# Feed-forward of a hybrid decoder: down products of two units in one PSUM sum, in two blocks per even unit

## The chip, the cores and the metric

The kernel runs on one core of a Trainium2 chip. Its time is device time in microseconds from the first to the last instruction, and what lies around it, of one execution. TensorE multiplies into PSUM (eight banks of 512 fp32 columns), VectorE, ScalarE and GpSimd do the element-wise work, and SyncE issues the DMAs. Each engine runs its own instructions in the order in which they are written and waits on semaphores.

## The reference, cut to what matters

The model layer is a token-mixing sub-layer and then the feed-forward (SwiGLU) that the change touches. T is 2056 tokens (2048 of the prompt, 8 samples), D is 1024, and the hidden width is 2816, 22 tiles of 128.

```python
h = _rmsnorm(x, g_pre_ffn) * (1.0 + sc_f) + sh_f
gate, up = jnp.split(jnp.einsum('btd,df->btf', h, w_ffn_in), 2, axis=-1)
f = jnp.einsum('btf,fd->btd', jax.nn.silu(gate) * up, w_ffn_out)
x = x + gt_f * _rmsnorm(f, g_post_ffn)
```

## The kernel before

The feed-forward is the last stage, `ffn`. Tokens stand in three groups of two halves (344, 342 and 342 tokens a half), and a group takes 22 **units**, one per tile of the hidden width, so units 0 to 65 in all; units 0 to 21 are group 0, 22 to 43 group 1, 44 to 65 group 2. The gate and up projections of a unit for both halves are made by a scheme of seven products instead of eight: `product` (L2094) does product j = 0 to 6 of a unit into the banks a, d, b, c, a, b, c, with 12 matmuls each, four chunks of the contraction times three terms of a high and a low part (`c_hi`, `c_lo` of the weights, `T_hi`, `T_lo` of the tokens).

What has to be ready for a product:

- VectorE makes four weight sums per unit, `s_add`: s3, s1, s2, s4 (L2269, L2272, L2276, L2280). ScalarE rounds each of the seven weight blocks to `c_hi` (`high_w`, L2137), GpSimd subtracts to get `c_lo` (`low_w`, L2034). Six buffers of each run ahead of TensorE.
- VectorE combines the products: `comb` (L2311) c11, u2, t, c22, u4, c21, c12. Product 5 writes bank b, so it waits for c11 of its own unit; product 6 waits for u2; product 4 waits for ScalarE's copy of product 0 (`first_product`); products 0 to 3 wait for t, u4, c21 and c12 of the unit ahead.
- ScalarE applies silu, VectorE multiplies (`gated`, L2317), ScalarE rounds to `f_hi` (`high_f`), VectorE makes `f_lo` (`low_f`, L2322). n is the half.
- The down weights of the unit are split the same way: `o_hi` on ScalarE (`high_o`, L2144), `o_lo` on GpSimd (`low_o`, L2039). Raw down weights have one buffer, loaded by SyncE when the `o_lo` ahead is done.

The down projection: unit d has 16 **tiles** y (eight rows of output tiles m, two halves n), each three matmuls into one of four banks Y (`tile`, L2112), which VectorE adds to `y` in SBUF (`collect`, L2339; a copy, L2337, for the first unit of a group). The tiles of unit d run in unit d+1, between the products (3, 3, 4, 3, 3 behind products 2 to 6). `spots` and `order`, built at the start of `ffn`, set this for all engines.

At a **turn** to the next group the new tokens h are loaded into the two buffers `E` and turned into seven `T` blocks in the last unit of the old group (t = 21, units 21 and 43) and the first of the new. In unit t = 1 of the new group there are no down tiles; instead the old group's `y` is squared into `E` (`squares`), summed by a tree on VectorE (`tree`), summed over partitions on TensorE (the two "sum" tiles), rooted on ScalarE (`root`), inverted, and scaled with `gate_f` (`scale`, L2394, eight instructions per half); then x is added (`output`, L2405) and SyncE stores the result. In t = 2 the tiles of two units run (6 behind most products). The same epilogue ends the kernel.

## Time and profile before

| | us |
|---|---|
| median of three runs | 2902.39 (2901.87 to 2910.81) |
| the profiled execution, its time | 2899.09 |
| its span, first to last instruction | 2897.0 |
| TensorE busy | 2566.6 (89%) |
| VectorE busy | 2109.5 (73%) |
| ScalarE busy | 1268.0 (44%) |
| GpSimd busy | 1270.5 (44%) |
| mean granted clock of TensorE | 0.953 of full speed |

The feed-forward starts its products at 1357 and ends its last tile at 2864, about half of the span. The busy time of TensorE counts a matmul until its modelled end, so two that overlap count once. An instruction's duration on VectorE, ScalarE and GpSimd includes the time in which it has been started and cannot yet proceed; the start of the next one lies up to 0.1 us ahead of its end.

### The profile page before, as it was taken

The numbers are of one execution on the slowest core, as the hardware profiler recorded it, in microseconds if no ns is written. First come the engines' busy times: TensorE is split into PE (matmuls) and PEld (weight loads), VectorE is DVE, ScalarE is ACT, GpSimd is POOL, SyncE is SP. The second block draws the span as 40 slices with busy tenths as digits, with TensorE's granted clock in tenths as the row PEclk, the third lists the DMA queues.
The fourth block names the chain that finished last, engine by engine and source line by source line (L and its number), as shares of the span: only waits on it lengthen the run. The fifth ranks groups of instructions, "written<-read, shape, count | busy, mean of one in ns | idle before, by whom it ended". The sixth has DMA issues, their size and how long they took to land. (4 is left out here: it accounts for less than half of the span.)

```text
span 2897.0 us, 43092 instructions
## 1 busy us (share of the span) xinstructions
PE 2566.6 (89%) x15492; PEld 2390.0 (83%) x15492; DVE 2109.5 (73%) x3246; ACT 1268.0 (44%) x2180; POOL 1270.5 (44%) x741
## 2 busy tenths in 40 slices
PE   5999999759888859995899999869999985999995
PEld 2999999647777747774899999759999975999995
DVE  2597789556767736744778777977777797777777
ACT  3556545357777744453333333423333342333332
POOL 1565566222323211001656555635656563555551
PEclk8999999979999979997999999989999998999997
DMA  5355344253333237953232222223222223222122
GB/s 217 117 174 168 130 149 168 80 123 94 79 101 95 57 100 214 278 170 113 79 106 83 71 79 75 71 103 119 74 81 73 81 66 107 81 66 88 67 74 85
DMA packets 199101, 315.40 MB, mean 109 GB/s; under 512 B 18210, under 2 KB 156194, under 8 KB 189938
## 3 DMA queue, kind: packets, MB, share of 16 engines
q1 hardware_dynamic: 174578, 295.80, 32.1%
q10 hardware_dynamic: 24320, 16.87, 2.2%
q8 instruction: 130, 2.13, 0.3%
q14 instruction: 73, 0.60, 0.1%
HBM read 266.29 MB, written 46.37 MB: 108 GB/s over the span
## 5 line engine op out<-in xcount | busy, mean ns | idle before, releaser
L2339 DVE TENSOR_TENSOR p_y<-p_y 128x342 f32<-128x342 f32 (+1 forms) x1008 | 462.6, 506 | 86.9 <-PE p_y L2112 86.9
L2034 POOL TENSOR_TENSOR p_c_lo<-ffn_wraw,p_c_hi 128x512 fp32r<-128x512 f32 x198 | 282.3, 1433 | 467.5 <-ACT p_c_hi L2137 467.5
L2034 POOL TENSOR_TENSOR p_c_lo<-p_graw,p_c_hi 128x512 fp32r<-128x512 f32 x198 | 275.1, 1396 | 324.4 <-ACT p_c_hi L2137 324.3
L2112 PE MATMUL p_y<-p_f_hi,p_o_hi 128*128 128x342 f32 (+1 forms) x1056 | 342.1, 324 | 72.1 <-DVE p_y L2337 48.3
L328 POOL TENSOR_TENSOR p_w_lo<-p_wraw,p_w_hi 128x1024 fp32r<-128x1024 f32 x100 | 294.9, 2958 | 212.2 <-ACT p_w_hi L389 211.9
L2112 PE MATMUL p_y<-p_f_hi,p_o_lo 128*128 128x342 f32 (+1 forms) x1056 | 340.5, 322 | 0.0
L2112 PE MATMUL p_y<-p_f_lo,p_o_hi 128*128 128x342 f32 (+1 forms) x1056 | 339.7, 322 | 0.0
L349 PE MATMUL p_proj<-p_h_hi,p_w_hi 128*128 128x412 f32 (+1 forms) x800 | 285.4, 357 | 15.3 <-POOL p_w_lo L328 15.2
L349 PE MATMUL p_proj<-p_h_lo,p_w_hi 128*128 128x412 f32 (+1 forms) x800 | 280.2, 350 | 0.0
L349 PE MATMUL p_proj<-p_h_hi,p_w_lo 128*128 128x412 f32 (+1 forms) x800 | 280.0, 350 | 0.0
L2112 PEld LDWEIGHTS p_y<-p_f_hi,p_o_hi 128*128 128x128 f32 x1056 | 201.3, 191 | 77.9 <-DVE p_y L2337 50.3
L2137 ACT ACTIVATE p_c_hi<-p_graw 128x512 fp32r<-128x512 f32 x198 | 120.2, 622 | 275.3 <-DVE p_graw L2276 197.7
L2137 ACT ACTIVATE p_c_hi<-ffn_wraw 128x512 fp32r<-128x512 f32 x198 | 120.2, 622 | 267.4 <-DVE ffn_wraw L2276 200.8
L2155 ACT ACTIVATE p_cg<-p_cg 128x342 f32<-128x342 f32 (+1 forms) x132 | 64.9, 491 | 322.8 <-DVE p_cg L2311 322.8
L2112 PEld LDWEIGHTS p_y<-p_f_lo,p_o_hi 128*128 128x128 f32 x1056 | 201.2, 191 | 0.0
L2112 PEld LDWEIGHTS p_y<-p_f_hi,p_o_lo 128*128 128x128 f32 x1056 | 201.2, 191 | 0.0
L2094 PE MATMUL p_a<-p_T_hi,p_c_hi 128*128 128x342 f32 (+1 forms) x528 | 171.5, 325 | 22.3 <-DVE p_T_lo L2364 16.4
L2322 DVE TENSOR_TENSOR p_f_lo<-p_cg,p_f_hi 128x342 fp32r<-128x342 f32 (+1 forms) x132 | 146.8, 1112 | 59.5 <-ACT p_f_hi L2162 59.5
L2039 POOL TENSOR_TENSOR p_o_lo<-ffn_wraw,p_o_hi 128x1024 fp32r<-128x1024 f32 x66 | 178.2, 2701 | 12.6 <-ACT p_o_hi L2144 12.6
L2094 PE MATMUL p_c<-p_T_hi,p_c_hi 128*128 128x342 f32 (+1 forms) x528 | 171.4, 325 | 9.1 <-POOL p_c_lo L2034 7.2
L2094 PE MATMUL p_b<-p_T_hi,p_c_hi 128*128 128x342 f32 (+1 forms) x528 | 170.2, 322 | 7.8 <-DVE p_cg L2311 6.1
L2094 PE MATMUL p_c<-p_T_lo,p_c_hi 128*128 128x342 f32 (+1 forms) x528 | 171.6, 325 | 0.0
(312 smaller groups left out, 7088.9 us busy)
## 6 DMA issues: line engine op xcount, KB each, us to landing
p_wraw<-w_in SPq DMA_DIRECT2D x100, 512.0 KB, 4.7
p_graw<-w_ffn SPq DMA_DIRECT2D x33, 1024.0 KB, 5.0
ffn_wraw<-w_ffn SPq DMA_DIRECT2D x65, 512.0 KB, 3.5
...
```

The source lines that it names most:

```text
L328: pool.tensor_tensor(w_lo[s][:], wraw[:, s, :], w_hi[s][:].bitcast(F32), ALU.subtract).then_inc(lo_done, 1)
L349: mm = pe.matmul(proj[n % 2][:, 0:W], a[n % RW][:, ks], b[g % 2][:, k, 0:W], start=i == 0, stop=i == 3 * KT - 1)
L2034: pool.tensor_tensor(c_lo[r][:], source(p), c_hi[r][:].bitcast(F32), ALU.subtract).then_inc(S["lo"], 1)
L2039: pool.tensor_tensor(o_lo[u % 2][:], oraw, o_hi[u % 2][:].bitcast(F32), ALU.subtract).then_inc(S["olo"], 1)
L2094: mm = pe.matmul(out[:, 0:W], a[r][:, k, :], b[j][:, k, 0:W], start=i == 0, stop=i == 11)
L2112: mm = pe.matmul(Y[q % YB][:, 0:W], a[s][:, m, :], b[s][:, n, 0:W], start=i == 0, stop=i == 2)
L2137: act.activation(c_hi[p % NR][:], source(p), ACT.Copy).then_inc(S["hi"], 1)
L2155: act.activation(cg[n][:, 0:W], cg[n][:, 0:W], ACT.Silu).then_inc(S["silu"], 1)
L2322: dve.tensor_tensor(f_lo[u % 2][:, n, 0:W], cg[n][:, 0:W], f_hi[u % 2][:, n, 0:W].bitcast(F32), ALU.subtract).then_inc(S["f"], 1)
L2339: dve.tensor_tensor(to, to, part, ALU.add).then_inc(S["yadd"], 1)
```

## The change

The down tiles of two units are one sum in PSUM: a tile of the pair u-2, u-1 is six matmuls in one bank, three per unit, and VectorE adds it to `y` once. All 16 tiles of a pair run in the even unit u, eight (half 0) behind product 5 and eight (half 1) behind product 6; an odd unit has none. The 16 tiles of the last pair run behind the last product. The high part of the down weights of an even unit is made at the start of the next unit, since its buffer is read until the end of the block; that of an odd unit is made ahead of `high_f`. At the turn, the two sums over partitions move behind products 3 and 6 of t = 1; the factor `gate_f` is taken to ScalarE (`gate`, eight instructions per half); `scale` is two VectorE instructions per half and `output` two; the first root moves behind the c_hi 2 of the next unit, the second root, inverse, scale and output go to t = 2; the two stores of y are issued in t = 1 and t = 2, one each.

```diff
     def pieces(u):
-        return [0, 2, 6, 6, 6, 6, 6] if len(downs(u)) == 2 else [0, 0, 3, 3, 4, 3, 3]
+        if u % 2 or not u:
+            return [0] * NPR
+        return [0, 0, 0, 0, 0, 8, 8]
...
+        pair = [("y", u - 2, n, m) for n in range(2) for m in range(KT)]
+        counts = pieces(u) if u < NU4 else [2 * KT]
+        for j, c in enumerate(counts):
+            spots[u, j] = list(range(len(order), len(order) + c))
+            order += pair[sum(counts[:j]):sum(counts[:j]) + c]
+            if u % FT == 1 and u > FT and j in (3, 6):
                 spots[u, j].append(len(order))
-                order.append(x)
...
+                order.append(("sum", group(u) - 1, (3, 6).index(j)))
...
                 if t == 0 and G:
                     for n in range(2):
                         load_x(G - 1, n)
-                    for n in range(2):
-                        store_y(G - 1, n)
+                if t in (1, 2) and G:
+                    store_y(G - 1, t - 1)
...
+                if u % 2:
+                    low_o(u - 1)
                 low_w(NPR * u + 5)
...
                 low_w(NPR * (u + 1) + 4)
-                low_o(u)
+                if u % 2:
+                    low_o(u)
...
-                    W, s = HW[group(d)], d % 2
-                    wait_f(pe, d, "lo", n)
-                    pe.wait_ge(S["olo"], d + 1)
-                    for i, (a, b) in enumerate(((o_hi, f_hi), (o_hi, f_lo), (o_lo, f_hi))):
-                        mm = pe.matmul(Y[q % YB][:, 0:W], a[s][:, m, :], b[s][:, n, 0:W], start=i == 0, stop=i == 2)
+                    W = HW[group(d)]
+                    for s in range(2):
+                        wait_f(pe, d + s, "lo", n)
+                        pe.wait_ge(S["olo"], d + s + 1)
+                        for i, (a, b) in enumerate(((o_hi, f_hi), (o_hi, f_lo), (o_lo, f_hi))):
+                            mm = pe.matmul(Y[q % YB][:, 0:W], a[s][:, m, :], b[s][:, n, 0:W], start=s == 0 and i == 0,
+                                           stop=s == 1 and i == 2)
...
+            def gate(G, n):
+                WP = HW[G] - (NS if G == NGR - 1 and n == 1 else 0)
+                act.wait_ge(S["sq"], 2 * G + n + 1)
+                for k in range(KT):
+                    ins = act.activation(y[:, k, n, 0:WP], y[:, k, n, 0:WP], ACT.Copy, scale=mods["gate_f"][:, k, 0:1])
+                ins.then_inc(S["gate"], 1)
...
-                high_o(u)
...
-                for k in range(KT):
-                    ins = dve.scalar_tensor_tensor(out=y[:, k, n, 0:WP], in0=y[:, k, n, 0:WP],
-                                                   scalar=mods["gate_f"][:, k, 0:1], in1=rstd[n][:, 0:WP],
-                                                   op0=ALU.mult, op1=ALU.mult)
...
+                dve.wait_ge(S["gate"], 2 * G + n + 1)
+                for k in (0, 4):
+                    dve.tensor_tensor(y[:, k:k + 4, n, 0:W], y[:, k:k + 4, n, 0:W],
+                                      rstd[n][:, 0:W].unsqueeze(1).broadcast_to((P, 4, W)), ALU.mult).then_inc(S["ep"], 1)
```

The line numbers of the changed kernel are a little higher: L2285 to L2296 are the weight sums (before L2269 to L2280), L2327 the combinations, L2333 the gate product, L2338 f_lo, L2353 the copies of y. On GpSimd the order of the instructions is the same in both kernels; what moves is what they wait for.

VectorE in a steady unit of group 0, from the gate product of half 0 (behind c21) on. Before:

```order
L2317 TENSOR_TENSOR p_cg<-p_cg,p_tt 128x344
L2339 TENSOR_TENSOR p_y<-p_y 128x344 x3
L2322 TENSOR_TENSOR p_f_lo<-p_cg,p_f_hi 128x344
L2311 TENSOR_TENSOR p_cg<-p_pu,p_c 128x344
L2339 TENSOR_TENSOR p_y<-p_y 128x344 x3
L2317 TENSOR_TENSOR p_cg<-p_cg,p_up 128x344
L2322 TENSOR_TENSOR p_f_lo<-p_cg,p_f_hi 128x344
L2280 TENSOR_TENSOR p_graw<-p_graw 128x512
L2269 TENSOR_TENSOR p_s<-ffn_wraw 128x512
L2339 TENSOR_TENSOR p_y<-p_y 128x344 x3
L2272 TENSOR_TENSOR ffn_wraw<-ffn_wraw 128x512
```

After, the same place in unit 2, whose tiles are the group's first and so copies:

```order
L2333 TENSOR_TENSOR p_cg<-p_cg,p_tt 128x344
L2353 COPY p_y<-p_y 128x344 x8
L2338 TENSOR_TENSOR p_f_lo<-p_cg,p_f_hi 128x344
L2327 TENSOR_TENSOR p_cg<-p_pu,p_c 128x344
L2353 COPY p_y<-p_y 128x344 x8
L2333 TENSOR_TENSOR p_cg<-p_cg,p_up 128x344
L2338 TENSOR_TENSOR p_f_lo<-p_cg,p_f_hi 128x344
L2296 TENSOR_TENSOR p_graw<-p_graw 128x512
L2285 TENSOR_TENSOR p_s<-ffn_wraw 128x512
L2288 TENSOR_TENSOR ffn_wraw<-ffn_wraw 128x512
L2327 TENSOR_TENSOR p_cg<-p_pu,p_b 128x344
```

The y instructions stand in two runs of eight behind the gate product and behind c12, and none are left between s3 and s1 or between the combinations.

ScalarE in a steady pair, from silu of half 0 on. Before, one unit:

```order
L2155 ACTIVATE p_cg<-p_cg 128x344
L2137 ACTIVATE p_c_hi<-p_graw 128x512 x3
L2162 ACTIVATE p_f_hi<-p_cg 128x344
L2137 ACTIVATE p_c_hi<-p_s 128x512
L2144 ACTIVATE p_o_hi<-ffn_wraw 128x1024
L2155 ACTIVATE p_cg<-p_cg 128x344
L2137 ACTIVATE p_c_hi<-p_graw 128x512
L2150 ACTIVATE p_pu<-p_a 128x344
```

After, from silu of half 0 of an even unit (no `o_hi` in it) to the start of the next:

```order
L2156 ACTIVATE p_cg<-p_cg 128x344
L2138 ACTIVATE p_c_hi<-p_graw 128x512 x3
L2163 ACTIVATE p_f_hi<-p_cg 128x344
L2138 ACTIVATE p_c_hi<-p_s 128x512
L2156 ACTIVATE p_cg<-p_cg 128x344
L2145 ACTIVATE p_o_hi<-ffn_wraw 128x1024
L2138 ACTIVATE p_c_hi<-p_graw 128x512
L2151 ACTIVATE p_pu<-p_a 128x344
L2163 ACTIVATE p_f_hi<-p_cg 128x344
L2138 ACTIVATE p_c_hi<-p_graw 128x512
```

`o_hi` of the even unit now stands behind the silu of the next unit's start, ahead of the c_hi 5, `p_pu` (product 0) and `f_hi` of half 1.

VectorE at the first turn, unit 23 (t = 1). Before, from s1 on:

```order
L2272 TENSOR_TENSOR ffn_wraw<-ffn_wraw 128x512
L2381 RECIPROCAL p_rstd<-p_rstd 128x344
L2311 TENSOR_TENSOR p_cg<-p_pu,p_b 128x342
L2311 TENSOR_TENSOR p_pu<-p_pu,p_c 128x342
L2394 SCALAR_TENSOR_TENSOR p_y<-p_y,gate_f,p_rstd 128x344 x8
L2311 TENSOR_TENSOR p_tt<-p_pu,p_a 128x342
L2311 TENSOR_TENSOR p_up<-p_tt,p_d 128x342
L2311 TENSOR_TENSOR p_pu<-p_pu,p_d 128x342
```

After, from t on, so with what stood there before further down:

```order
L2327 TENSOR_TENSOR p_tt<-p_pu,p_a 128x342
L2327 TENSOR_TENSOR p_up<-p_tt,p_d 128x342
L2327 TENSOR_TENSOR p_pu<-p_pu,p_d 128x342
L2397 RECIPROCAL p_rstd<-p_rstd 128x344
L2292 TENSOR_TENSOR ffn_wraw<-ffn_wraw 128x512
L2327 TENSOR_TENSOR p_tt<-p_tt,p_b 128x342
L2333 TENSOR_TENSOR p_cg<-p_cg,p_tt 128x342
L2404 TENSOR_TENSOR p_y<-p_y,p_rstd 128x4x344 x2
L2338 TENSOR_TENSOR p_f_lo<-p_cg,p_f_hi 128x342
L2418 TENSOR_TENSOR p_E<-p_E,p_y 128x1376 x2
L2327 TENSOR_TENSOR p_cg<-p_pu,p_c 128x342
```

The inverse and the scaling of half 0 move from around c11 and u2 to behind u4 and the gate product; the scaling is two instructions, the output two.

## Rows read from the trace of the kernel before

**Rows 1.** Page, the span in 40 equal slices: TensorE's busy tenths.

```profile
PE   5999999759888859995899999869999985999995
```

**Rows 2.** Windows: length, busy us (instructions) per engine, clock, DMA share, GB/s.

```profile
1812.82:1869.58 56.76, 46.27 (x265) 45.16 (x265) 50.48 (x71) 23.54 (x34) 34.16 (x19) 0.91 0.16 56
1869.58:1948.44 78.86, 48.07 (x270) 45.01 (x269) 62.88 (x91) 25.24 (x36) 34.13 (x18) 0.85 0.34 116
2321.85:2378.28 56.43, 46.00 (x265) 44.87 (x265) 50.51 (x71) 23.56 (x34) 34.21 (x19) 0.91 0.16 57
2378.28:2461.66 83.38, 47.17 (x270) 44.13 (x269) 62.74 (x90) 25.08 (x36) 33.98 (x18) 0.84 0.39 109
2461.66:2482.35 20.69, 20.69 (x134) 20.69 (x133) 15.65 (x32) 6.25 (x12) 9.65 (x8) 1.00 0.18 63
2355.04:2378.28 23.24, 21.29 (x134) 20.75 (x133) 22.83 (x35) 10.77 (x17) 16.86 (x11) 1.00 0.21 70
```

**Rows 3.** Waits of TensorE, 1200 to 2897: us in total, times, longest.

```profile
PE p_y L2112 <- DVE p_y L2337: 48.3, 6, 13.5
```

**Rows 4.** Timeline of VectorE, first turn: start, us, what, [idle before <-releaser].

```profile
1834.85 2.88 DVE L2364 TENSOR_TENSOR p_T_lo<-p_E,p_T_hi 128x1368 fp32r<-128x1368 f32 x1 [2.19 <-ACT p_T_hi L2175]
...
1859.64 0.50 DVE L2311 TENSOR_TENSOR p_cg<-p_pu,p_b 128x342 f32<-128x342 f32 x1
...
1885.43 0.45 DVE L2311 TENSOR_TENSOR p_cg<-p_pu,p_b 128x342 f32<-128x342 f32 x1
...
1886.41 6.05 DVE L2394 SCALAR_TENSOR_TENSOR p_y<-p_y,gate_f,p_rstd 128x344 f32<-128x344 f32 x8
...
1922.89 0.69 DVE L2269 TENSOR_TENSOR p_s<-p_graw 128x512 f32<-128x512 f32 x1 [8.43 <-DMA p_graw<-w_ffn]
```

**Rows 5.** Timeline of SyncE's queue, first turn.

```profile
1900.98 13.24 SPq L2004 DMA_DIRECT2D yT<-p_E  x2
```

**Rows 6.** Timeline of VectorE, a steady unit of group 2.

```profile
2515.56 0.51 DVE L2311 TENSOR_TENSOR p_tt<-p_pu,p_a 128x342 f32<-128x342 f32 x1 [1.35 <-PE p_a L2094]
...
2517.01 1.76 DVE L2339 TENSOR_TENSOR p_y<-p_y 128x342 f32<-128x342 f32 x4
```

**Rows 7.** Timeline of ScalarE, the same stretch.

```profile
2505.21 0.46 ACT L2150 ACTIVATE p_pu<-p_a 128x342 f32<-128x342 f32 x1 [1.22 <-PE p_a L2094]
...
2520.49 0.49 ACT L2162 ACTIVATE p_f_hi<-p_cg 128x342 fp32r<-128x342 f32 x1 [0.39 <-DVE p_cg L2317]
...
2520.89 0.62 ACT L2137 ACTIVATE p_c_hi<-p_s 128x512 fp32r<-128x512 f32 x1
...
2521.41 1.04 ACT L2144 ACTIVATE p_o_hi<-ffn_wraw 128x1024 fp32r<-128x1024 f32 x1
```

**Rows 8.** Timeline of TensorE, first matmul of a steady unit.

```profile
2503.12 0.32 PE L2094 MATMUL p_a<-p_T_hi,p_c_hi 128*128 128x342 f32 x1
```

**Rows 9.** Timeline, VectorE and GpSimd (POOL) side by side in unit 1.

```profile
1398.53 2.67 POOL L2039 TENSOR_TENSOR p_o_lo<-ffn_wraw,p_o_hi 128x1024 fp32r<-128x1024 f32 x1
...
1399.64 1.94 DVE L2322 TENSOR_TENSOR p_f_lo<-p_cg,p_f_hi 128x344 fp32r<-128x344 f32 x1 [0.69 <-ACT p_f_hi L2162]
...
1401.17 1.56 POOL L2034 TENSOR_TENSOR p_c_lo<-p_graw,p_c_hi 128x512 fp32r<-128x512 f32 x1
...
1401.51 1.77 DVE L2280 TENSOR_TENSOR p_graw<-p_graw 128x512 f32<-128x512 f32 x1
...
1403.20 0.68 DVE L2269 TENSOR_TENSOR p_s<-ffn_wraw 128x512 f32<-128x512 f32 x1
```

**Rows 10.** Timeline of GpSimd (POOL), a steady unit of group 2.

```profile
2513.05 2.54 POOL L2034 TENSOR_TENSOR p_c_lo<-ffn_wraw,p_c_hi 128x512 fp32r<-128x512 f32 x2 [2.42 <-ACT p_c_hi L2137]
```

**Rows 11.** Timeline of TensorE, unit 23, product 5.

```profile
1886.02 0.40 PE L2094 MATMUL p_b<-p_T_hi,p_c_hi 128*128 128x342 f32 x1 [2.37 <-DVE p_cg L2311]
```

**Rows 12.** Timeline of VectorE at the end of the kernel.

```profile
2864.82 1.58 DVE L2370 TENSOR_TENSOR p_E<-p_E 128x1368 f32<-128x1368 f32 x1
...
2873.04 3.98 DVE L2394 SCALAR_TENSOR_TENSOR p_y<-p_y,gate_f,p_rstd 128x342 f32<-128x342 f32 x8
```

More of the change, by code:

```diff
@@ L1888, in ffn @@
         if x[0] == "y":
-            done[x[1]], done[x[1], x[2]] = q + 1, q + 1
+            for d in (x[1], x[1] + 1):
+                done[d], done[d, x[2]] = q + 1, q + 1
     with ExitStack() as ctx:
@@ L1925, in ffn @@
         E_LOADS = {("h", 0): 1, ("h", 1): 2, ("x", 0): 3, ("h", 2): 4, ("x", 1): 5, ("x", 2): 6}
-        S = {n: sem(n) for n in ("prod", "tile", "hi", "ohi", "p1", "silu", "fhi", "thi", "sq", "root", "s_add", "comb", "f",
+        S = {n: sem(n) for n in ("prod", "tile", "hi", "ohi", "p1", "silu", "fhi", "thi", "sq", "gate", "root", "s_add", "comb", "f",
                                  "yadd", "t_dve", "ep", "lo", "olo", "t_pool")}
@@ L2215, in _ @@
                     squares(G - 1, 1)
+                if G and t == 2:
+                    root(G - 1, 1)
                 first_product(u)
@@ L2229, in _ @@
                 if G and t == 1:
-                    root(G - 1, 0)
+                    gate(G - 1, 0)
                 silu(u, 0)
@@ L2239, in _ @@
                     high_t(turn, 3)
+                if G and t == 1:
+                    root(G - 1, 0)
                 high_w(NPR * (u + 1) + 3)
@@ L2242, in _ @@
                     high_t(turn, 4)
-                if G and t == 1:
-                    root(G - 1, 1)
+                if u % 2:
+                    high_o(u)
                 high_f(u, 0)
                 high_w(NPR * (u + 1) + 4)
-                high_o(u)
+                if G and t == 1:
+                    gate(G - 1, 1)
                 if turn:
@@ L2255, in _ @@
                 squares(NGR - 1, n)
+                gate(NGR - 1, n)
             for n in range(2):
@@ L2404, in output @@
                 dve.wait_ge(e_in[n], 16 * E_LOADS["x", G])
-                dve.tensor_tensor(E[n][:, :, 0:W], E[n][:, :, 0:W], y[:, :, n, 0:W], ALU.add).then_inc(S["ep"], 1)
+                if G == NGR - 1 and n == 1:
+                    ys = y[:, :, n, W - NS:W]
+                    dve.tensor_tensor(ys, ys, mods["gate_f"][:, :, 1:C9], ALU.mult).then_inc(S["ep"], 1)
+                    wait_ep(dve, G, f"part{n}")
+                    dve.tensor_tensor(E[n][:, :, 0:W], E[n][:, :, 0:W], y[:, :, n, 0:W], ALU.add).then_inc(S["ep"], 1)
+                else:
+                    for k in (0, 4):
+                        dve.tensor_tensor(E[n][:, k:k + 4, 0:W], E[n][:, k:k + 4, 0:W], y[:, k:k + 4, n, 0:W], ALU.add
+                                          ).then_inc(S["ep"], 1)
             low_t(0, 0)
@@ L2429, in _ @@
                     inverse(late, 1)
-                    scale(late, 1)
                 collect(u, 0)
@@ L2441, in _ @@
                 if late is not None:
-                    output(late, 1)
+                    scale(late, 1)
                 collect(u, 1)
@@ L2453, in _ @@
                 s_add(u + 1, "s1")
-                if ends is not None:
-                    inverse(ends, 0)
+                if late is not None:
+                    output(late, 1)
                 comb(u, "c11")
@@ L2462, in _ @@
                     low_t(0, 6)
-                if ends is not None:
-                    scale(ends, 0)
                 comb(u, "t")
@@ L2467, in _ @@
                 comb(u, "u4")
+                if ends is not None:
+                    inverse(ends, 0)
                 collect(u, 4)
@@ L2473, in _ @@
                 gated(u, 0)
+                if ends is not None:
+                    scale(ends, 0)
                 collect(u, 5)
```

34 lines of the change are left out of this document (7 added, 27 removed).

## The prediction

> **What bounds the kernel now.** I read the span in slices first: TensorE is busy in nine tenths or more of most of the second half, where the feed-forward runs, with two dents [rows 1]. The windows say how full: a steady unit of group 2 takes 20.69 us, TensorE and its weight load are both busy for all 20.69 us, at a granted clock of 1.00 [rows 2]. A unit has 84 matmuls for seven products and 48 for the down tiles, so one takes 20.69/132 = 0.157 us. Nothing that VectorE saves can shorten such a unit. What can be gained is in the two dents, the turns from one token group to the next. The four units of the first turn (21 to 24) take 56.76 + 78.86 = 135.6 us, those of the second 56.43 + 83.38 = 139.8 us [rows 2], against 4 x 20.75 = 83 us of TensorE work. The largest waits there are the 48.3 us for the copies of the new group's first tiles, which stand on VectorE behind the outputs of the old group [rows 3]. Between the copies VectorE waited 8.43 us for weights [rows 4], whose load SyncE could issue only after it had stood in two stores of y for 13.24 us [rows 5].
>
> **Work that stays and work that goes.** TensorE does the same matmuls: 528 tiles of six for 1056 of three. The 528 removed VectorE additions at 0.42 us from start to start (four from 2517.01, the last ending at 2518.77 with 0.08 us of overlap [rows 6]) are some 220 us of an engine that a steady unit does not wait for: worth nothing by themselves. In an even unit (from here w) all tiles stand behind products 5 and 6, so a unit is no longer an even 20.7 us: an odd unit v is 84 x 0.157 = 13.2 us, an even one 180 x 0.157 = 28.2 us. VectorE, ScalarE and GpSimd still have the same preparation per unit, and until now the tiles gave it time. So I follow the preparation through a pair, with 0 at the first matmul of v. A product starts every 1.88 us, and its result can be used 2.09 us after its first matmul (2503.12 to 2505.21 [rows 7, 8]).
>
> **The pair, step by step.** VectorE and GpSimd stand in each other's way: f_lo takes 1.94 us where o_lo runs on GpSimd, and ends 0.4 us after it. The weight sum that follows (L2280) takes 1.77 us beside a c_lo, against 0.68 us for its neighbour [rows 9]. In the Trainium skill, "SBUF — State Buffer", section "Who interferes with whom", such an instruction with two SBUF inputs waits for the whole GpSimd instruction, and one with a PSUM input does not. By that the removed additions (one PSUM input each) give GpSimd nothing; if they had shared its port, some 0.4 us a tile would have come back to it, which the sum here does not hold.
> ScalarE splits o of the last even unit at 0.2 to 1.2 (1.04 us [rows 7]), GpSimd makes its o_lo until 3.7 (2.67 us in a row that begins with some 0.3 us of waiting [rows 9]). f_lo ends at 4.1, s4 (behind a c_lo) at 5.8, s3 and s1 follow, and c11 of v is there at 7.6. TensorE wants it for product 5 at 5 x 1.88 = 9.4: cover of 1.8 us. The result of product 4 comes at 9.6; t, c22 and u4 follow, and s2 starts 1.45 us later, at 11.1 (2515.56 to 2517.01 [rows 6]). GpSimd is then inside a run of four c_lo, 1.25 us each (two in 2.54 [rows 10]), until 12.0, so s2 ends at 12.5. c21 and the gate product follow (13.6), on ScalarE c_hi 3, o_hi of v (1.04 us, now ahead of f_hi) and f_hi (14.6), then c_hi 4 (15.1); on VectorE f_lo (15.1) and c12 (15.6). silu ends at 16.1, the second gate product waits for c_lo 4 (16.8), and o_lo of v runs until 19.1. From the end of an o_lo to c11 the rows give 2.0 us (1401.20 to 1403.20 [rows 9]) and then s3, s1 and c11, 1.8 us: c11 of w is there at 22.9, and TensorE starts 0.14 us after it (1885.88 to 1886.02 [rows 4, 11]), at 23.0. It wants it at 12 x 1.88 = 22.6. So **0.4 us are lost in each pair**, and what hides the rest of the chain is used up. 28 of the 32 even units with tiles are outside the turns: 28 x 0.4 = +11 us. The bounds: 0 us where s2 slips in ahead of the c_lo (then c11 comes 1.1 us earlier), and 1.1 us a pair where one more c_lo (1.25 us) gets in ahead of s1: 0 to +31 us. Within w the tiles come every 0.94 us and VectorE needs 0.42 for one, so four banks are enough.
>
> **The turns.** First half, units 21 and 22. VectorE bounds them already, with the new group's T. In front of c11 of unit 22 (it ends at 1860.1, 47.3 us after the start of 21 [rows 2, 4]) 19 y adds go, 19 x 0.42 = 8.0 us. But part of them filled waits for ScalarE's T_hi (2.19 us before T_lo at 1834.85 [rows 4]), and f_lo and s4 at the start of 21 now meet o_lo (2.4 us more); following the chain as above, c11 comes at 45 us. Now, though, all 96 tile matmuls and products 5 and 6 stand behind it: 120 x 0.157 = 18.9 us, where 9.5 us stood (56.76 less 47.3). The clock adds to this: TensorE is busy for 46.27 us in the first half [rows 2], where 264 matmuls at 0.157 are 41.4, so 4.8 us go at half clock. I take 1.5 of them behind c11. This is 65.5 us for 56.6: +9 us in each turn.
> Second half, units 23 and 24. What goes: the load is no longer behind the second store, the copies stand behind products 5 and 6, and scaling changes from eight instructions of 6.05 us in all [rows 4] to two, for which the nearest row is an add of the same size, 1.58 us [rows 12], so 3.2 us and a c_lo of 1.25 on top. What comes: eight ScalarE instructions per half (8 x 0.40 = 3.2 us, from start to start as f_hi at 2520.49 and what follows it at 2520.89 [rows 7]), which put the first root from 16 to 19 us. The chain is then: c11 of 23 at 15.5; root at 19, reciprocal 2.3, s2, c21, gate product, scale 4.4, f_lo, output 4.3 with a c_lo: c12 at 32; second root at 35, reciprocal 2.3, f_lo, s4, scale 4.4, s3, s1, output 4.3: c11 of 24 at 49.3. With 18.9 us of TensorE work and 1.8 at half clock that is 70 us, for 78.86 and 83.38: -9 and -13 us. **Both turns together: 9 + 9 - 9 - 13 = -4 us.** The bounds: -25 us, where the 8 us of adds and the scales' 3 us come out in full in every half; +15 us, where each wait meets one more c_lo on its way.
>
> **Start and end.** Units 0 and 1 keep their order but for the tiles, which units 1 and 2 exchange: 0. At the end the root waits 3.2 us for the gate copies, of which the squares' sum hid half, and two scales save 2 x (3.98 - 3.16) [rows 12]: 0.
>
> **Sum.** 11 - 4 + 0 = +7 us on the profiled execution of 2899.09 us, which is 3.3 us below the median; on the median, 2902.4 + 7 = 2909 us. A measurement of this kernel can tell some 0.3% (8.7 us) from no change.
>
> **Rivals.**
> Forecast, about no change (2894 to 2911): the shortfall of 0.4 us a pair and turns that give a little. For it speaks that every piece has a row; against it that it is a difference of two long chains. Chance 0.40.
> Slower: one mechanism, the wait of product 5 in each even unit for c11, which stands on VectorE behind o_lo. If one c_lo more gets in, the loss is 1.1 to 1.6 us a pair: 28 x 1.4 = 39, less 4: 2937 us. It decides from (8.7 + 4)/28 = 0.45 us a pair on. For it speaks that two c_lo and an o_lo lie in the chain and each missed turn costs 1.25 us; against it that s1 is ready 0.15 us before the next c_lo. Chance 0.30.
> Faster: steady pairs lose nothing and the turns give 25 us, since VectorE, busy for 62.88 of 78.86 us there [rows 2], gets rid of its adds and long scales: 2878 us. For it speaks that half of the wait at the turns was for a load that comes earlier now; against it that tiles at the end of a unit no longer fill TensorE's waits. Chance 0.25.
> Slower still: the clock. From 2355.04 to 2378.28 TensorE was idle for 23.24 - 21.29 = 1.95 us in short pieces, at a clock of 1.00 [rows 2], so short waits did not cost it there. If a wait in each pair does bring it down, at half of the 4.8 us from above for each, it is 28 x 2.4 = 67 us: 2974 us. Chance 0.05. "TensorE: Matmul & The Clock Gate", section "A second HAM failure mode: psum-queue depth-cycling" of the Trainium skill, describes such a clock that swings with small idle times between groups; no row here shows it.
>
> **Chances.** Faster 0.25, same 0.40, slower 0.35. The range has to reach to both neighbours: 2878 to 2942 us.
>
> **What would show it.** Right: even units of about 28.6 us with TensorE's wait for p_cg (c11) of 0.4 us at product 5; odd units of 13.2 us without a wait; units 21 and 22 together 65 us, 23 and 24 together 70 us; VectorE's busy time down by some 250 us. Wrong: a wait of over 1 us a pair, or none; a wait in odd units (for c_lo 5 or s1); turns under 120 us; a clock under 1.00 in a steady stretch.

## The result: 0.3% slower, and where the time went

The changed kernel takes 2912.95 us (median, 2906.52 to 2917.46) against 2902.31 us (2896.56 to 2910.81) of the kernel before: the ratio is 1.0034, with a 95% interval of 1.0026 to 1.0042. The forecast was 2909 us, with 2878 to 2942 us as its range. The difference, 10.6 us, is a little more than the 8.7 us that the prediction called the smallest that a measurement of this kernel can tell from none, and the interval leaves no doubt of its sign. The median lies 2 us above the band that the prediction gave its likeliest case (2894 to 2911 us). One of the five executions of the kernel e4_unpaired below took 4333.8 us at a granted clock of 0.554; its ratio is that of the other four, whose median is 2935.58 us.

The page of the changed kernel begins as follows (span; busy us of each engine; TensorE's busy tenths in 40 slices, which answer to [rows 1]):

```profile
span 2912.4 us, 42580 instructions
...
PE 2581.5 (89%) x15492; PEld 2401.1 (82%) x15492; DVE 2018.1 (69%) x2686; ACT 1289.3 (44%) x2228; POOL 1297.5 (45%) x741
...
PE   5999999759888959995999999779999977999995
```

VectorE does 560 instructions less and TensorE is no better used. The windows below answer to [rows 2] (length, busy us of TensorE, its weight load, VectorE, ScalarE and GpSimd with instructions, granted clock, DMA share, GB/s): units 21 and 22, units 23 and 24, the same of the second turn, then an odd and an even steady unit.

```profile
1821.56:1884.91 63.35, 46.52 (x265) 45.47 (x265) 48.42 (x55) 25.29 (x34) 34.92 (x18) 0.87 0.15 50
1884.91:1955.48 70.57, 49.54 (x270) 48.39 (x269) 57.90 (x62) 30.20 (x49) 30.54 (x16) 0.83 0.32 105
2336.19:2399.58 63.39, 45.80 (x266) 44.79 (x265) 48.33 (x55) 25.27 (x34) 34.61 (x18) 0.89 0.16 51
2399.58:2470.39 70.81, 50.64 (x270) 49.49 (x269) 57.83 (x62) 30.16 (x49) 30.49 (x16) 0.81 0.33 104
2470.39:2483.66 13.27, 13.27 (x87) 13.27 (x85) 9.45 (x14) 5.63 (x10) 9.35 (x6) 1.00 0.67 155
2483.66:2512.59 28.93, 28.54 (x181) 28.28 (x181) 20.84 (x33) 8.57 (x17) 15.53 (x10) 1.00 0.26 88
```

A steady pair is 13.27 + 28.93 = 42.20 us, where two units took 41.49 us before (2482.35 to 2523.84, start to start). By stretches, from the start of unit 1 to the last instruction of each profiled execution, in us:

| stretch | before | after | difference | predicted |
|---|---|---|---|---|
| units 1 to 20 | 416.46 | 422.37 | +5.9 | |
| units 25 to 42 | 373.41 | 380.71 | +7.3 | |
| units 47 to 64 | 373.41 | 379.76 | +6.4 | |
| steady, together | | | +19.6 | +11 |
| units 21+22, 43+44 | 56.76, 56.43 | 63.35, 63.39 | +13.5 | +18 |
| units 23+24, 45+46 | 78.86, 83.38 | 70.57, 70.81 | -20.9 | -22 |
| unit 65 to the end | 61.93 | 62.25 | +0.3 | 0 |
| sum | 1500.64 | 1513.21 | +12.6 | +7 |

Ahead of unit 1 the code is unchanged but for the place of o_hi and o_lo of unit 0; in the profiled executions of all kernels of this study unit 1 begins between 1392.2 and 1401.9 us, so the 2.8 us by which it begins later here lie within that spread and are not counted to the change.

TensorE's waits in the feed-forward, which answer to [rows 3] (us in total, times, longest):

```profile
PE p_b L2093 <- DVE p_cg L2327: 63.5, 37, 10.4
PE p_c L2093 <- DVE p_cg L2327: 21.7, 4, 6.0
PE p_a L2093 <- DVE p_tt L2327: 3.3, 2, 1.8
```

The 48.3 us of waits for copies are gone entirely. In their place stand waits of product 5 (bank b) for c11, 37 of them: one in each of the 28 steady even units, eight at the turns and one in unit 0. At the turns there are also four of product 3 (bank c) for c12.

### The profile page after: what moved, and what is told of

It reads as the page before. It is cut to its first block and busy times, and to the rows that moved or that the text cites. A ratio compares the mean times of both kernels' runs of the same rounds, so it can differ in the third digit from the quotient of the medians.

```text
span 2912.4 us, 42580 instructions
## 1 busy us (share of the span) xinstructions
PE 2581.5 (89%) x15492; PEld 2401.1 (82%) x15492; DVE 2018.1 (69%) x2686; ACT 1289.3 (44%) x2228; POOL 1297.5 (45%) x741
## 5 line engine op out<-in xcount | busy, mean ns | idle before, releaser
L2030 POOL TENSOR_TENSOR p_c_lo<-ffn_wraw,p_c_hi 128x512 fp32r<-128x512 f32 x198 | 285.8, 1456 | 293.5 <-ACT p_c_hi L2138 293.5
L2355 DVE TENSOR_TENSOR p_y<-p_y 128x342 f32<-128x342 f32 (+1 forms) x480 | 237.2, 509 | 145.1 <-PE p_y L2112 143.2
L2030 POOL TENSOR_TENSOR p_c_lo<-p_graw,p_c_hi 128x512 fp32r<-128x512 f32 x198 | 302.6, 1548 | 62.2 <-ACT p_c_hi L2138 62.2
L2093 PE MATMUL p_b<-p_T_hi,p_c_hi 128*128 128x342 f32 (+1 forms) x528 | 176.7, 335 | 65.1 <-DVE p_cg L2327 63.5
L2338 DVE TENSOR_TENSOR p_f_lo<-p_cg,p_f_hi 128x342 fp32r<-128x342 f32 (+1 forms) x132 | 142.6, 1080 | 105.6 <-ACT p_f_hi L2163 103.3
L2093 PE MATMUL p_c<-p_T_hi,p_c_lo 128*128 128x342 f32 (+1 forms) x528 | 173.5, 329 | 0.0
```

Of the source, the lines that this page charges most:

```text
L2030: pool.tensor_tensor(c_lo[r][:], source(p), c_hi[r][:].bitcast(F32), ALU.subtract).then_inc(S["lo"], 1)
L2093: mm = pe.matmul(out[:, 0:W], a[r][:, k, :], b[j][:, k, 0:W], start=i == 0, stop=i == 11)
L2338: dve.tensor_tensor(f_lo[u % 2][:, n, 0:W], cg[n][:, 0:W], f_hi[u % 2][:, n, 0:W].bitcast(F32), ALU.subtract).then_inc(S["f"], 1)
L2355: dve.tensor_tensor(to, to, part, ALU.add).then_inc(S["yadd"], 1)
```

## Experiments

All medians are beside runs of the kernel before on the same chip. "Pair" is an odd and an even steady unit of the later groups (two units where the tiles are spread over both). Units are given for the first turn and the second.

| kernel | median, us | ratio, 95% interval | pair, us | 21+22, 43+44 | 23+24, 45+46 |
|---|---|---|---|---|---|
| changed | 2912.95 | 1.0034 (1.0026 to 1.0042) | 42.20 | 63.35, 63.39 | 70.57, 70.81 |
| e1_olo_late | 2918.24 | 1.0057 (1.0044 to 1.007) | 42.27 | 64.78, 64.83 | 70.28, 69.59 |
| e9_short_olo | 2892.69 | 0.9975 (0.9963 to 0.9986) | 41.57 | 62.48, 62.52 | 68.83, 68.56 |
| e4_unpaired | 2936.35 | 1.012 (1.0103 to 1.0136) | 43.11 | 63.50, 63.40 | 68.13, 68.02 |
| e2_tiles_early | 2883.68 | 0.9941 (0.9927 to 0.9956) | 41.50 | 61.33, 61.35 | 66.93, 66.84 |
| e8_no_gate | 2882.95 | 0.9944 (0.993 to 0.9958) | 41.50 | 61.31, 60.96 | 67.77, 67.50 |
| e6_old_tiles | 2886.35 | 0.9957 (0.9944 to 0.9971) | 41.49 | 56.81, 56.46 | 70.25, 71.69 |
| e5_before_stores | 2878.01 | 0.9921 (0.9908 to 0.9934) | 41.49 | 56.79, 56.37 | 69.75, 69.12 |
| e13_four_ahead | 2873.92 | 0.9894 (0.9878 to 0.9911) | 41.49 | 56.77, 56.38 | 68.05, 68.17 |
| e10_pairs_at_turn | 2862.26 | 0.9865 (0.9848 to 0.9882) | 41.49 | 56.77, 56.44 | 62.44, 62.27 |
| e11_late_epilogue | 2877.10 | 0.9917 (0.9903 to 0.9932) | 41.49 | 56.80, 56.38 | 69.90, 69.71 |
| e12_tiles_later | 2853.54 | 0.9844 (0.983 to 0.9858) | 41.49 | 56.75, 56.38 | 58.05, 59.47 |

### The steady pair: o_lo placed later

```diff
                 low_w(NPR * u + 6)
+                if u and u % 2 == 0:
+                    low_o(u - 1)
...
                 low_w(NPR * (u + 1) + 4)
-                if u % 2:
-                    low_o(u)
+            low_o(NU4 - 1)
```

> The changed kernel, with o_lo of the odd unit placed behind c_lo 6 of the even unit instead of behind c_lo 4 made for it, so that f_lo (half 1) and s4 no longer stand behind it on the way to c11. Theory (the steady loss is the wait of product 5 for c11, and o_lo is what makes c11 late): c11 of the even unit is there at about 21 to 22 us of a pair, wanted at 22.6; the wait of 0.39 us is gone, a pair takes 41.6 us instead of 42.2, and 28 pairs give 17 us: about 2896 us. Rival (the o_lo meets another instruction with two SBUF inputs on the same way, such as s3 or s1, and the wait stays): 2913 us within 4. If only the wait goes and the rest of the excess is in the blocks themselves: 28 x 0.4 = 11 us, 2902 us.

It got slower: 2918.24 us. The first half of the theory came true, the second not. VectorE, GpSimd and TensorE in the even unit that starts at 2534.16:

```profile
2541.25 0.50 DVE L2328 TENSOR_TENSOR p_cg<-p_pu,p_b 128x342 f32<-128x342 f32 x1
...
2546.21 1.69 DVE L2293 TENSOR_TENSOR p_graw<-p_graw 128x512 f32<-128x512 f32 x1 [0.95 <-POOL p_c_lo L2030]
...
2549.35 2.31 DVE L2356 TENSOR_TENSOR p_y<-p_y 128x342 f32<-128x342 f32 x5
```

```profile
2542.44 2.42 POOL L2035 TENSOR_TENSOR p_o_lo<-ffn_wraw,p_o_hi 128x1024 fp32r<-128x1024 f32 x1
2544.80 5.76 POOL L2030 TENSOR_TENSOR p_c_lo<-p_graw,p_c_hi 128x512 fp32r<-128x512 f32 x4
```

```profile
2549.90 0.42 PE L2113 MATMUL p_y<-p_f_hi,p_o_hi 128*128 128x342 f32 x1 [0.52 <-DVE p_y L2356]
```

c11 ends at 2541.75, 20.85 us into the pair (21 to 22 expected), and product 5 no longer waits. But s2 waits for GpSimd (0.95 us, for a c_lo) and starts 12.05 us into the unit, and the first addition of the block starts at 15.19. In the changed kernel these are 11.94 and 15.01 us, so VectorE's row hardly moved, while TensorE now begins the block 11.26 us into the unit instead of 11.89. The fifth tile wants a bank that the first addition has to free, and now waits 0.52 us. The wait moved from the front of the block into it.

### The steady pair: o_lo made short

```diff
-                pool.tensor_tensor(o_lo[u % 2][:], oraw, o_hi[u % 2][:].bitcast(F32), ALU.subtract
-                                   ).then_inc(S["olo"], 1)
+                part = slice(0, 1) if u % 2 and u > 1 else slice(0, KT)
+                pool.tensor_tensor(o_lo[u % 2][:, part, :], oraw[:, part, :], o_hi[u % 2][:, part, :].bitcast(F32),
+                                   ALU.subtract).then_inc(S["olo"], 1)
```

> The changed kernel in which o_lo of the odd units is made for one of its eight blocks only (about 0.35 us of GpSimd instead of 2.67 us; the other seven keep the values of unit 1, so that part of the output leaves out the low part of the down weights as it should be); nothing else is changed. Theory (the loss of 0.63 to 0.7 us in each steady pair is GpSimd's o_lo, which makes either c11 or, where it stands later, the first addition late): c11 of the even unit at about 20.7 us of a pair, no wait at product 5 and none in the block, 41.55 us a pair, about 18 us less than the changed kernel: 2895 us. Rival (VectorE's own row of instructions is too long between the start of the even unit and the first addition, whatever GpSimd does): a wait in the block of 0.4 us or more stays, 2908 us or more.

2892.69 us (2895 expected). A steady pair, columns as in the windows above:

```profile
2447.09:2488.66 41.57, 41.57 (x266) 41.57 (x265) 27.86 (x46) 14.19 (x26) 22.69 (x16) 1.00 0.41 110
```

TensorE is busy for the whole pair: no wait at product 5 and none in the block. With the run before this one it says that the wait of a steady pair is the odd unit's o_lo, 2.67 us of GpSimd in front of f_lo and s4 or in front of s2. In neither of the two places tried for it are both c11 and the first addition on time, with all tiles behind product 5; other places were not tried.

### The order without the sum

```diff
-        return [0, 0, 0, 0, 0, 8, 8]
+        return [0, 0, 0, 0, 0, 16, 16]
...
-        pair = [("y", u - 2, n, m) for n in range(2) for m in range(KT)]
+        pair = [("y", d, n, m) for n in range(2) for d in (u - 2, u - 1) for m in range(KT)]
```

(and `tile` makes three matmuls of one unit again.)

> The changed kernel with tiles of three matmuls again, 16 behind product 5 and 16 behind product 6 of the even unit, each added by VectorE: the order of the change without the sum of two units. Theory A (the additions that the pairing saves are hidden in a steady pair, as the 0.157 us for each of 132 matmuls said, and cost only at the turns): about 2913 + 2 x 7 = 2927 us. Theory B (with tiles of 0.47 us the four banks are full 1.9 us after the block begins, while VectorE comes to the first addition only at 28.3 us of the pair, 3.1 us after the block's start; so TensorE waits about 1.8 us in each pair): 2913 + 28 x 2 + 14 = about 2983 us. So the two-unit sum and the blocks would be worth something only together.

2936.35 us: between the two theories. A pair takes 43.11 us, 0.9 us more than with the sum; the wait is in the block, as Theory B had it, and of about the size that it named, 1.45 us for 1.8. That theory forgot that the wait at product 5 (0.39 us in the profile) goes when the block is longer: the steady units have none here, and c11 is there 22.1 us into the pair, not 23.0.

```profile
2509.01 0.43 PE L2111 MATMUL p_y<-p_f_hi,p_o_hi 128*128 128x342 f32 x1 [1.45 <-DVE p_y L2353]
```

So in blocks at the end of a unit the sum is worth some 23 us. That is a balance: the steady stretches are 27.7 us longer without it, but units 23+24 and 45+46 are 2.4 and 2.8 us shorter (68.13 and 68.02 for 70.57 and 70.81), where both theories took the missing sum to cost time; why was not followed. In the steady pairs the sum repairs a loss that the blocks make; against tiles spread over the unit it gains nothing there (41.49 us without blocks and without sums).

### The same tiles, four of them ahead of product 5

```diff
-        return [0, 0, 0, 0, 0, 8, 8]
+        return [0, 0, 0, 2, 2, 6, 6]
```

> The changed kernel with the tiles of the even unit as 2, 2, 6 and 6 behind products 3, 4, 5 and 6, instead of 8 and 8 behind 5 and 6: TensorE has 24 matmuls (3.8 us) more to do before product 5 wants c11. Theory: the steady wait goes (28 x 0.6 = 17 us), and at the turns four tiles fill 3.8 us of the waits of 1.1 and 10.4 us for c11 (1 + 4 us in each turn, 10 us in both): about 2886 us. Rival (what counts is VectorE's chain at the turns, which gets four additions more ahead of t and s2): the steady gain alone, about 2896 us. Rival (the steady excess isn't the wait): above 2903 us.

2883.68 us (2886 expected), 0.6% faster than the kernel before. Units 21+22, units 23+24, and a steady pair:

```profile
1814.10:1875.43 61.33, 46.31 (x266) 45.54 (x265) 47.24 (x55) 25.40 (x34) 34.34 (x18) 0.86 0.16 52
1875.43:1942.36 66.93, 49.90 (x270) 48.74 (x269) 56.66 (x62) 30.19 (x49) 30.29 (x16) 0.85 0.34 111
2457.21:2498.71 41.50, 41.50 (x267) 41.50 (x266) 30.20 (x46) 14.18 (x27) 24.25 (x16) 1.00 0.32 103
```

The 24 matmuls ahead of product 5 cover c11, the pair has no wait, and the turns are 2.0 us (21+22) and 3.6 us (23+24) shorter, since TensorE has tiles while it waits. VectorE's instructions are the same in number: only places changed.

### The stores alone

```diff
                 if t == 0 and G:
                     for n in range(2):
                         load_x(G - 1, n)
-                    for n in range(2):
-                        store_y(G - 1, n)
+                if t in (1, 2) and G:
+                    store_y(G - 1, t - 1)
```

> The kernel before, with the two stores of y issued in t = 1 and t = 2, behind the loads of the weights, as in the changed kernel; nothing else is changed. Theory (at the turn the copies wait for s3, and s3 for a load that SyncE issues behind the second store): VectorE's waits of 8.4 and 14.1 us for the load go, and the two units t = 1 and 2 take 71 and 70 us for 78.9 and 83.4: about 2902 - 20 = 2882 us. So the turns' gain of the change (8.3 and 12.6 us in those units) would come from the stores alone. Rival (behind the load another wait is late, c_hi and c_lo of the next unit): a gain of under 10 us, 2893 us or more.

2878.01 us: 22.8 us less than before, by two DMA instructions put elsewhere. Units 23+24 and 45+46, and the place on VectorE at which it waited 8.43 us for the load [rows 4]:

```profile
1869.75:1939.50 69.75, 46.87 (x270) 44.22 (x269) 63.04 (x91) 25.03 (x36) 34.50 (x18) 0.90 0.35 110
2369.31:2438.43 69.12, 49.21 (x270) 46.73 (x269) 62.93 (x91) 24.99 (x36) 34.47 (x18) 0.88 0.36 109
```

```profile
1914.14 0.50 DVE L2337 COPY p_y<-p_y 128x342 f32<-128x342 f32 x1
1914.56 0.92 DVE L2269 TENSOR_TENSOR p_s<-p_graw 128x512 f32<-128x512 f32 x1
```

s3 follows the copy with no wait. The two stretches are 9.1 and 14.3 us shorter than before, and 0.8 and 1.7 us shorter than in the changed kernel. So this line alone is enough for all that the change gained at the turns (20.9 us; the line gives 23.4). The changed kernel with the stores in their old place was not run.

### The change's epilogue with the tiles of before

Changed kernel; `pieces`, `order`, `tile`, `high_o` and `low_o` as before:

```diff
-        return [0, 0, 0, 0, 0, 8, 8]
+        return [0, 2, 6, 6, 6, 6, 6] if len(downs(u)) == 2 else [0, 0, 3, 3, 4, 3, 3]
...
-                if u % 2:
-                    low_o(u)
+                low_o(u)
```

> The changed kernel with the tiles of the kernel before: tiles of three matmuls of one unit, 3, 3, 4, 3, 3 behind products 2 to 6 of the next unit, both o_hi and o_lo in their old places; the epilogue (sums, gate on ScalarE, roots, scale, output, stores) stays as changed. Theory (the change's epilogue is good for the turns and its tiles are bad for them and for the steady pairs): pairs of 41.5 us, units 21+22 56.8 us as before, units 23+24 about 66 us: 41.49 x 28 and turns of 123 us, 6 us less than with the stores alone: about 2872 us. Rival (the epilogue gives nothing beyond the stores, since VectorE adds 32 tiles again in t = 2): 2878 to 2882 us. Rival (the tiles of two units cost the turns, not the place of the tiles): units 23+24 at 70 us as in the changed kernel, 2880 us.

2886.35 us: the first rival, and a little worse than it (2878 to 2882). Units 21+22 take 56.81 us, so the 6.6 and 7.0 us that the change loses there come from its tiles and the places of o_hi and o_lo that go with them. Units 23+24 take 70.25 us, no less than with the stores alone, and the stretch from unit 65 to the end is 3.4 us longer than there, which was not followed. The second root now stands in t = 2 and holds a bank of the tiles:

```profile
1905.52 0.66 PE L2113 MATMUL p_y<-p_f_hi,p_o_hi 128*128 128x342 f32 x1 [8.20 <-ACT p_rstd L2202]
```

### The factor gate_f back on VectorE

Kernel with 2, 2, 6, 6, without `gate`:

```diff
-                for k in (0, 4):
-                    dve.tensor_tensor(y[:, k:k + 4, n, 0:W], y[:, k:k + 4, n, 0:W],
-                                      rstd[n][:, 0:W].unsqueeze(1).broadcast_to((P, 4, W)), ALU.mult).then_inc(S["ep"], 1)
...
+                for k in range(KT):
+                    ins = dve.scalar_tensor_tensor(out=y[:, k, n, 0:WP], in0=y[:, k, n, 0:WP],
+                                                   scalar=mods["gate_f"][:, k, 0:1], in1=rstd[n][:, 0:WP],
+                                                   op0=ALU.mult, op1=ALU.mult)
...
```

> The kernel with tiles 2, 2, 6, 6 behind products 3 to 6, with the scaling by gate_f back on VectorE (eight instructions per half, none on ScalarE). Theory (the gate copies on ScalarE hide nothing that VectorE would have had to do later: two scales save 0.9 us each in clean time, and the first root comes up to 1.2 us later for them): the same as the kernel with the gate copies, 2884 us within 3. Rival (ScalarE's factor is what shortens the second half of the turn): 2 turns x 4 us, 2892 us.

2882.95 us, the same as 2883.68 within the intervals. Units 23+24 take 67.77 us for 66.93, and the stretch from unit 65 to the end 61.56 us for 61.95: a small gain at each turn that the end gives back in part.

### The sum only where VectorE is the bound

Two kernels, both from the one with the stores moved. The first:

```diff
-        return [0, 2, 6, 6, 6, 6, 6] if len(downs(u)) == 2 else [0, 0, 3, 3, 4, 3, 3]
+        return [0, 1, 3, 3, 3, 3, 3] if len(downs(u)) == 2 else [0, 0, 3, 3, 4, 3, 3]
...
-        todo = [("y", d, n, m) for d in downs(u) for n in range(2) for m in range(KT)]
+        todo = [("y", d, n, m) for d in downs(u)[:1] for n in range(2) for m in range(KT)]
```

(and a tile of unit 22 or 44 is six matmuls, three of it and three of the unit behind it.)

> The kernel before with the stores moved, and the sum of two units only in the two units t = 2 of the turns (units 24 and 46), where the tiles of t = 0 and t = 1 run together: 1, 3, 3, 3, 3, 3 tiles of six matmuls behind products 1 to 6 instead of 2, 6, 6, 6, 6, 6 of three. Everywhere else a tile is one unit. Theory (the sum is worth something only where VectorE, not TensorE, sets the end): in a turn 16 additions of 0.43 us go (some of them hidden behind TensorE), and the four banks hold 3.8 us of TensorE work instead of 1.9 us when it comes to wait for the first copy: units t = 1 and 2 take 66 us instead of 69.6, 6 to 7 us in all: about 2872 us. Rival (behind the first copy TensorE's own work sets the end, and the additions are hidden here too): 1.9 us a turn or less, 2874 to 2878 us.

2862.26 us, ratio 0.9865: more than expected, 15.7 us less than with the stores alone. Unit 24 there, then here:

```profile
1893.20:1939.50 46.30, 31.67 (x180) 30.50 (x181) 40.24 (x63) 13.61 (x22) 22.04 (x12) 0.85 0.23 70
```

```profile
1894.38:1933.36 38.98, 31.07 (x180) 30.26 (x181) 32.73 (x48) 11.65 (x19) 19.28 (x10) 0.91 0.24 77
```

VectorE is busy for 7.5 us less (15 instructions), and the unit is 7.3 us shorter. The second kernel keeps the places and leaves the sum out:

```diff
-        return [0, 2, 6, 6, 6, 6, 6] if len(downs(u)) == 2 else [0, 0, 3, 3, 4, 3, 3]
+        return [0, 1, 3, 7, 7, 7, 7] if len(downs(u)) == 2 else [0, 0, 3, 3, 4, 3, 3]
```

> The kernel before with the stores moved, and the 32 tiles of t = 2, still of three matmuls each, as 1, 3, 7, 7, 7, 7 behind products 1 to 6 instead of 2, 6, 6, 6, 6, 6: the same four tiles stand ahead of product 3 as in the run with pairs at the turn, and only the sum of two units is missing. That run gained 15.7 us on the moved stores, against 6 to 7 expected. Theory A (the removed additions did it: behind the first copy VectorE has 32 of 0.43 us and some 9 us of other work, 23 us, against 17 us of TensorE work; so VectorE sets the end here and 16 additions are 7 us a turn): this run gains 0 to 2 us a turn, 2874 to 2878 us. Theory B (the places did it: TensorE makes product 3 while it waits, and starts less cold): 2862 to 2866 us.

```profile
1895.45:1940.03 44.58, 32.11 (x181) 29.89 (x182) 39.76 (x63) 13.61 (x22) 22.53 (x12) 0.89 0.24 75
```

2873.92 us. Of the 7.3 us, 1.7 are the places and 5.6 the sum (in unit 46: 0.9 of 6.8, and 5.9). So Theory A holds for the greater part. But the sum does two things here: it takes 16 additions away, and it lets the four banks hold twice the TensorE work while VectorE is in the epilogue. VectorE starts its first copy 20.5 us into unit 24 in all three kernels. When TensorE gets its next bank, it has done 48 of the unit's 180 matmuls with the stores alone, 60 here and 78 with the pairs, and with the pairs the last 102 then run in 16.2 us with no wait. The 18 matmuls more are 18 x 0.157 = 2.8 us of the 5.6; how the gain splits between the banks and the additions is not shown.

### Moving the late epilogue, twice

First, inverse, scale and output of half 1 behind u4, with the pairs as above:

```diff
-                if late is not None:
-                    inverse(late, 1)
-                    scale(late, 1)
...
-                if late is not None:
-                    output(late, 1)
...
                 comb(u, "u4")
+                if late is not None:
+                    inverse(late, 1)
+                    scale(late, 1)
+                    output(late, 1)
                 collect(u, 4)
```

> As the run with pairs at the turn only, and inverse, scale and output of half 1 (10.2 us on VectorE in t = 2) stand behind u4 instead of ahead of the first copies, s3, s1 and c11. Theory (what TensorE waits for at the turn is the place of the epilogue on VectorE, not its amount): TensorE gets copies and c11 ten us earlier, works on for 18 us and then waits about 8 us for the copies behind the output; units t = 1 and 2 take 58 to 60 us, 7 us less in each turn: about 2859 us. Rival (VectorE sets the end of the unit anyway, and the wait only moves behind the output): 0 to 2 us a turn, 2869 us or more.

2877.10 us: the gain of the pairs was lost again. VectorE, and TensorE behind it:

```profile
1911.43 0.52 DVE L2344 COPY p_y<-p_y 128x342 f32<-128x342 f32 x1 [2.46 <-PE p_y L2118]
...
1921.41 2.29 DVE L2388 RECIPROCAL p_rstd<-p_rstd 128x344 f32<-128x344 f32 x1
```

```profile
1931.27 0.65 PE L2118 MATMUL p_y<-p_f_hi,p_o_hi 128*128 128x342 f32 x1 [5.66 <-DVE p_y L2344]
```

TensorE stood at its first tile for o_lo of unit 23 until 1906, VectorE idled for the tiles from 1909 on, and the epilogue that could have filled this began at 1921. Neither of the two accounts in the expectation had that wait in it. The last kernel was made from this reading: tiles only behind products 3 to 6, so that TensorE makes products 2 and 3 while o_lo is due, the inverse in its old place, and scale and output behind the copies of half 0:

```diff
-        return [0, 1, 3, 3, 3, 3, 3] if len(downs(u)) == 2 else [0, 0, 3, 3, 4, 3, 3]
+        return [0, 0, 0, 4, 4, 4, 4] if len(downs(u)) == 2 else [0, 0, 3, 3, 4, 3, 3]
...
                 collect(u, 4)
+                if late is not None:
+                    scale(late, 1)
+                    output(late, 1)
```

> As the run with pairs at the turn only (2862 us), with the tiles of t = 2 as 4, 4, 4, 4 behind products 3 to 6 instead of 1, 3, 3, 3, 3, 3 behind 1 to 6, so that TensorE makes products 2 and 3 while it has to wait for o_lo of unit t = 1 (7.3 and 5.7 us), and with scale and output of half 1 behind the eight copies of half 0 (behind u4 and the tiles of product 4); the inverse stays where it was. Theory (in the run with the late epilogue the order on VectorE was right, but TensorE stood at the first tile for o_lo, VectorE idled for the copies meanwhile, and the epilogue began 12 us too late): units 24 and 46 take 33 us instead of 39, 12 us in both: about 2851 us. Rival (the wait for the copies of half 1 behind the output takes the gain back, as in that run): 2862 us or more.

2853.54 us, ratio 0.9844 (0.983 to 0.9858): 1.6% faster than the kernel before and the fastest of the study. Units 24 and 46:

```profile
1890.39:1925.00 34.61, 30.62 (x181) 29.84 (x181) 31.12 (x48) 11.65 (x19) 17.63 (x10) 0.96 0.28 87
2378.21:2414.29 36.08, 32.27 (x180) 31.50 (x181) 31.32 (x48) 11.65 (x19) 17.58 (x10) 0.91 0.28 84
```

33 us were expected; a wait of 2.0 us for the copies behind the output is left in each. Tiles and epilogue were moved together here, so what each gave is not shown.

## Why the prediction was right, and where it was not

**The steady bound** was right: two units without waits are 41.49 us before, and every kernel with no wait in them comes to 41.49 to 41.57 us, whether VectorE adds 32 tiles in them or, as in e2_tiles_early (41.50), 16.

**The pair, step by step** was right to 0.2 us at each step. The pair that begins at 2512.59, VectorE, GpSimd and TensorE:

```profile
2515.56 1.19 DVE L2338 TENSOR_TENSOR p_f_lo<-p_cg,p_f_hi 128x342 fp32r<-128x342 f32 x1 [1.83 <-ACT p_f_hi L2163]
...
2523.72 1.52 DVE L2292 TENSOR_TENSOR ffn_wraw<-ffn_wraw 128x512 f32<-128x512 f32 x1
...
2530.12 2.07 DVE L2338 TENSOR_TENSOR p_f_lo<-p_cg,p_f_hi 128x342 fp32r<-128x342 f32 x1 [0.56 <-ACT p_f_hi L2163]
2532.11 1.78 DVE L2296 TENSOR_TENSOR ffn_wraw<-ffn_wraw 128x512 f32<-128x512 f32 x1
...
2535.13 0.50 DVE L2327 TENSOR_TENSOR p_cg<-p_pu,p_b 128x342 f32<-128x342 f32 x1
```

```profile
2513.99 2.39 POOL L2035 TENSOR_TENSOR p_o_lo<-ffn_wraw,p_o_hi 128x1024 fp32r<-128x1024 f32 x1 [8.18 <-ACT p_o_hi L2145]
...
2529.15 2.67 POOL L2035 TENSOR_TENSOR p_o_lo<-ffn_wraw,p_o_hi 128x1024 fp32r<-128x1024 f32 x1
```

```profile
2535.07 0.32 PE L2093 MATMUL p_a<-p_T_hi,p_c_lo 128*128 128x342 f32 x1
2535.78 0.40 PE L2093 MATMUL p_b<-p_T_hi,p_c_hi 128*128 128x342 f32 x1 [0.39 <-DVE p_cg L2327]
```

Counted from 2512.59, with the prediction's figure behind it: f_lo ends at 4.16 (4.1), s2 ends at 12.65 (12.5, in the run of c_lo as foretold), the o_lo of the odd unit ends at 19.23 (19.1), c11 of the even unit at 23.04 (22.9), TensorE starts product 5 at 23.19 (23.0). The wait has the place and the cause that were predicted, and e9_short_olo shows that the cause is that o_lo. That the profile lists it with 0.39 us, where 0.4 was predicted, is a coincidence: the prediction's 0.4 ran from the start that TensorE wanted to the start that it got, and that is 0.55 us.

**The term that was mis-sized is what such a wait costs.** The pair is 0.70 us longer, not 0.4. From the start of the last matmul ahead of the wait to the start of product 5 are 0.71 us where 0.157 is the pace, so 0.55 us are lost; the first step behind it is 0.24 us (2535.78 to 2536.02), which is 0.08 more. Together that is 0.63 us for a wait that is listed with 0.39, since the listed idle time begins at the modelled end of the last matmul (0.32 us long at a pace of 0.157). The last 0.08 us are no wait: e9_short_olo has them too (41.57 for 41.49), and their cause is open. Of the prediction's two times, the start wanted (12 x 1.88 = 22.56) came 0.08 us later, at 22.64, and the start got (23.0) 0.19 us later. In group 0 a pair is 0.54 us longer (42.16 for 41.62). So 28 pairs cost 19.6 us and not 11. These 8.6 us were partly made up by luck: the turns gave 3.3 us more than their term, so the whole is +12.6 us in the profiled executions and +10.6 in the medians, for +7. The stated range of 64 us also held the times of the rivals Slower (2937) and Faster (2878), so that the time lies in it says little; the steps above say more.

**The turns.** First half: c11 of unit 22 ends 44.3 us behind the start of 21 (45 predicted), and 63.35 us for 65.5. Second half: c11 of 23 at 14.7 us (15.5), the first root ends at 18.1 (19), c12 at 33.2 (32), the second root at 36.1 (35), c11 of 24 at 49.3 (49.3), 70.57 us for 70. The turns together give 7.3 us for 4. The working held; what it did not tell was which of its pieces the gain came from. It named the load, the scales and the additions together. The stores alone give 9.1 and 14.3 us there, more than all of the change; the rest of the new epilogue gives nothing that shows (e6_old_tiles, e8_no_gate). The sum of two units is worth 5.6 and 5.9 us in units 24 and 46 (e10_pairs_at_turn against e13_four_ahead), where the tiles do not stand in blocks at the end; in the blocks it costs time at the turns (e4_unpaired).

**The end** was right (0.3 us).

**VectorE's busy time** was the sign that failed: down by 91.4 us and not 250. The additions went (462.6 us for 1008 of them before, 237.2 us for 480 after), but s2 (L2292, before L2276) and s4 (L2296, before L2280) now stand beside GpSimd in every unit. Groups of VectorE, after and before (count, busy us, mean ns, idle before):

```profile
L2296 DVE TENSOR_TENSOR p_graw<-p_graw 128x512 f32<-128x512 f32 x33 | 56.4, 1709 | 0.0
L2292 DVE TENSOR_TENSOR p_graw<-p_graw 128x512 f32<-128x512 f32 x33 | 50.1, 1517 | 0.0
```

```profile
L2280 DVE TENSOR_TENSOR p_graw<-p_graw 128x512 f32<-128x512 f32 x33 | 23.5, 712 | 0.0
L2276 DVE TENSOR_TENSOR p_graw<-p_graw 128x512 f32<-128x512 f32 x33 | 22.6, 684 | 0.0
```

With the other half of each, 206.7 us for 92.1: 114.6 us of waiting, counted as busy. Such collisions are in the prediction's chain (s4 behind a c_lo, s2 inside the run of c_lo); the total was made from the removed work alone and left them out.

**The rivals.** Slower: its mechanism (one more c_lo ahead of s1) did not come about, but its threshold of 0.45 us a pair was passed by the forecast's own mechanism at its true price, so the result lies on the border of the two. Faster: the steady pairs had to lose nothing; in e2_tiles_early they do, and the kernel is faster. The clock: 1.00 in the steady windows with a wait in each pair, so that rival fell. A rule that the prediction cited, "SBUF — State Buffer", "Who interferes with whom" in the Trainium skill, says that a VectorE instruction with at most one SBUF input, as a y addition is, does not contend with GpSimd. The trace of the kernel before agrees: from 1400 us on, 62 c_lo of p_graw meet y additions and nothing else on VectorE and take 1.29 us in the mean, as the 55 that meet nothing. With 528 additions fewer c_lo takes 1456 and 1548 ns in the mean, not less than the 1434 and 1396 before; more of them now meet a weight sum or an f_lo, and those that meet nothing still take 1.29 us.
